# Fewer filler matmuls on TensorE at eight places of a two-layer diffusion block

## The reference

```python
for layer in range(DEPTH):                                   # DEPTH = 2
    mod_l = silu(c) @ w_mod[layer] + b_mod[layer]            # six vectors: shift, scale, gate, twice
    y_l, y_c = mixer(modulate(x, sh1, sc1), modulate(ctx, csh1, csc1), w_in[layer], ...)
    x = post_norm(x, g1 * y_l, ln1_w[layer], ln1_b[layer])
    x = post_norm(x, g2 * swiglu(modulate(x, sh2, sc2), w_gate_up[layer], w_down[layer]), ...)
    # the context tokens likewise, in layer 0 only
# mixer: h @ w_in, split into global attention, window attention, Fourier mixing, retention;
#        their results side by side, @ w_out
# modulate(x, shift, scale) = layer_norm(x) * (1 + scale) + shift
# post_norm(x, y, w, b) = layer_norm(ALPHA * x + y, w, b)
```

## Time and profile before

| | |
|---|---|
| median of 3 runs | 1728.65 us (1728.42 to 1732.66) |
| the profiled execution | 1728.65 us, of which the span is 1726.8 us |
| TensorE busy | 1648.3 us, 95% |
| GpSimd, VectorE, ScalarE busy | 853.3, 826.3, 454.1 us |
| mean granted TensorE clock | 0.992 |
| mean DMA rate | 94 GB/s |

### The profile page before, as it was taken

How to read it: one execution, slowest core, us unless ns; L and a number is a source line. 1 busy time by engine, 2 the same in 40 slices (tenths; PEclk the granted TensorE clock), 3 DMA queues, 4 the chain that set the end, 5 groups by cost and what they waited for, 6 DMA issues and landing times. The chain is left out here.

```text
span 1726.8 us, 23654 instructions
## 1 busy us (share of the span) xinstructions
PE 1648.3 (95%) x9480; PEld 1391.7 (81%) x9480; DVE 826.3 (48%) x1236; ACT 454.1 (26%) x945; POOL 853.3 (49%) x840
## 2 busy tenths in 40 slices
PE   6999999999899999999999999999999999999997
PEld 4877866767899987899998788786768888688885
DVE  4353254647772415444445684635477421520048
ACT  5511465423500021100003164126433300210021
POOL 4443143623464443544444581523475577587772
PEclk9999999999999999999999999999999999999999
DMA  9212043311353312244642120210013542233321
GB/s 359 76 50 73 2 130 129 109 57 53 98 159 98 110 43 67 64 144 120 198 159 76 67 74 25 73 50 8 26 52 98 147 146 92 92 98 98 98 85 49
DMA packets 157010, 161.98 MB, mean 94 GB/s; under 512 B 6382, under 2 KB 111966, under 8 KB 156646
## 3 DMA queue, kind: packets, MB, share of 16 engines
q1 hardware_dynamic: 136566, 121.40, 22.8%
q10 hardware_dynamic: 20336, 39.08, 6.9%
HBM read 158.36 MB, written 2.10 MB: 93 GB/s over the span
## 5 line engine op out<-in xcount | busy, mean ns | idle before, releaser
L675 POOL TENSOR_SCALAR ring_hi<-stage 128x512 fp32r<-128x512 f32 x352 | 247.9, 704 | 621.4 <-PE ps L745 595.0
L678 POOL TENSOR_TENSOR ring_lo<-stage,ring_hi 128x512 fp32r<-128x512 f32 x352 | 490.0, 1392 | 29.4
L743 PE MATMUL ps<-act_hi,ring_hi 128*128 128x384 f32 (+2 forms) x1088 | 379.9, 349 | 0.0
L745 PE MATMUL ps<-act_hi,ring_lo 128*128 128x384 f32 (+2 forms) x1088 | 378.3, 348 | 0.0
L744 PE MATMUL ps<-act_lo,ring_hi 128*128 128x384 f32 (+2 forms) x1088 | 378.2, 348 | 0.0
L743 PE MATMUL ps<-ring_hi,act_hi 128*128 128x512 f32 (+1 forms) x700 | 280.7, 401 | 11.6 <-DVE act_lo L1872 5.4
L745 PE MATMUL ps<-ring_hi,act_lo 128*128 128x512 f32 (+1 forms) x700 | 273.3, 390 | 0.0
L744 PE MATMUL ps<-ring_lo,act_hi 128*128 128x512 f32 (+1 forms) x700 | 273.1, 390 | 0.0
L745 PEld LDWEIGHTS ps<-act_hi,ring_lo 128*128 128x128 f32 x1088 | 204.6, 188 | 13.2
L743 PEld LDWEIGHTS ps<-act_hi,ring_hi 128*128 128x128 f32 x1088 | 204.7, 188 | 13.0
L744 PEld LDWEIGHTS ps<-act_lo,ring_hi 128*128 128x128 f32 x1088 | 204.7, 188 | 12.9
(11 more groups left out here) (258 smaller groups left out, 2123.3 us busy)
## 6 DMA issues: line engine op xcount, KB each, us to landing
stage<-in_w_gate_up_dram SPq DMA_DIRECT2D x88, 512.0 KB, 5.1
mod_stage<-in_w_mod_dram ACTq DMA_DIRECT2D x56, 512.0 KB, 4.4
stage<-in_w_in_dram SPq DMA_DIRECT2D x18, 1024.0 KB, 5.0
stage<-in_w_down_dram SPq DMA_DIRECT2D x16, 1024.0 KB, 4.9
stage<-in_w_mod_dram SPq DMA_DIRECT2D x12, 1024.0 KB, 5.2
start_mod<-in_w_mod_dram SPq DMA_DIRECT2D x8, 1024.0 KB, 12.3
stage<-in_w_down_dram SPq DMA_DIRECT2D x8, 768.0 KB, 4.4
stage<-in_w_out_dram SPq DMA_DIRECT2D x16, 256.0 KB, 4.5
```

Source lines behind the costliest of these rows:

```text
L675: nc.gpsimd.tensor_scalar(hi_, stage[:, par, j * 512:(j + 1) * 512], 1.0, 0.0, ALU.mult, ALU.add).then_inc(w_hi, 1)
L678: nc.gpsimd.tensor_tensor(lo_, stage[:, par, j * 512:(j + 1) * 512], hi_.bitcast(F32), ALU.subtract).then_inc(w_ready, 1)
L743: nc.tensor.matmul(o, a_hi, b_hi, start=first, stop=False)
L745: return nc.tensor.matmul(o, a_lo, b_hi, start=False, stop=last)
```

## The change

The counts of all eight fillers are cut: 30 to 10, 28 to 10, 18 to 5, 44 to 10 twice, 28 to 8, 30 to 8, 44 to 16. In layer 1's attention the filler also waits for the second exponential instead of the first, and writes bank 7 instead of bank 5. In all, 266 fillers become 77. No other instruction changes on any engine.

```diff
@@ project
                             if n == 0 and j in (4, 7):
-                                keep_clock(1, 44)
+                                keep_clock(1, 10)
...
                 if l == 0:
-                    keep_clock(2, 30)
+                    keep_clock(2, 10)
@@ attention
                     if s == 2 and l == DEPTH - 1:
-                        need(pe, "probs_ready", l, 1)
-                        keep_clock(5, 28)
+                        need(pe, "probs_ready", l, 2)
+                        keep_clock(7, 8)
...
                     if s == 1 and l < DEPTH - 1:
-                        keep_clock(6, 28)
+                        keep_clock(6, 10)
...
                     if s == 2 and l < DEPTH - 1:
-                        keep_clock(6, 18)
+                        keep_clock(6, 5)
@@ gate_up
                     for n in ([1, 2] if n_parts == 2 else []):
-                        keep_clock(0, (30, 44)[n - 1])
+                        keep_clock(0, 8 * n)
                         transposes(key, n)
```

## The result

The changed kernel took 1741.41 us (median of 7 runs, 1737.09 to 1743.81), the kernel before 1732.11 us beside it (7 runs, 1727.55 to 1732.83). The ratio is 1.0057 with a 95% interval of 1.004 to 1.0075: slower, by 9.3 us between the medians. The forecast was 1734.2 us with a range of 1729 to 1739. The direction was right; the size and the range were not.

The account below looks back on a forecast made before the run. The prediction took the kernel as bound by TensorE, busy 95% of the span. Terms of 1.2, 0.7, 0.6, 1.1, 1.8 and 0.2 summed to 5.6 us on 1728.65, giving 1734.2 us, range 1729.0 to 1739.0.

Parts of the forecast that it names:

- No gain from fewer fillers: At all eight places, 189 fillers fewer save 21 us of TensorE work, which all turn into idle time.
- A fall at each place: Clock falls expected at start, both attentions and project; gate_up falls already, with little new there.
- rival 1: Only long gaps lower the clock, so start and attention hold; project 1.8 and gate_up 0.2 remain: 1730.7 us, chance 0.28.
- 3 (nothing happens): Rival: the few fillers suffice at every place, 1728.7 us, chance 0.07.
- Rival 4: Three VectorE steps on the norm chains (project, gate_up) get 0.7 us shorter each: 1726.5 us, chance 0.05.
- start: Program start, 20 fillers fewer, 2.7 us idle: a fall into dense matmuls adds 1.2 us, from 0 to 3.2.
- layer 0's attention: Two gaps, 2.6 and 1.9 us idle: slower scores on the path add 0.7 and 0.6 us, 0 to 1.6 each.
- layer 1's project: Two gaps, 4.5 and 5.2 us idle: slower transposes and products add 1.8 us, from 0.4 to 3.
- layer 1's attention: Two idle pieces of about 1.8 us: a fall into the scores at 1179.35 adds 1.1 us, from 0 to 1.6.
- gate_up: Gaps of 3.1 and 5.3 us idle, the second's fall already present and hidden: adds 0.2 us, from -0.3 to 1.
- what a fall costs: A fall wholly in dense matmuls costs 1.6 us; one over a tile's eight transposes costs 0.7 us.
- Rival 2: Low clock stays longer: start, project and one attention gap meet two low stretches each, 4.8 us more: 1739 us, chance 0.10.

Follow-up runs that it names:

- e3_project: Kernel before with only layer 1's project fillers cut (44 to 10, twice): 1734.88 us, ratio 1.0007.
- e8_gates: Kernel before with the gate broadcasts cut into two pieces, a weight slot's products between them: 1738.95 us, ratio 1.004.
- f1_changed: The changed kernel run again beside the kernel before: 1740.0 us, ratio 1.0042.
- e1_start: Kernel before with only the filler at the program's start cut (30 to 10): 1734.47 us, ratio 1.0004.
- e2_att0: Kernel before with only layer 0's attention fillers cut (28 to 10, 18 to 5): 1735.47 us, ratio 1.0011.
- e5_gateup: Kernel before with only layer 1's gate_up fillers cut (30 to 8, 44 to 16): 1733.49 us, ratio 1.0006.
- e6_more: Kernel before with more fillers at each of the eight places, such as 30 to 33 and 44 to 62: 1733.02 us, ratio 1.0007.
- e4_att1: Kernel before with only layer 1's attention filler changed (28 to 8, bank 7, behind the second exponential): 1733.41 us, ratio 1.0002.

## Why the prediction was wrong, and where it was right

**No gain from fewer fillers: right where the clock was up.** Behind every shortened filler the same engine ended the wait. Its working missed one case: when the clock is already low, 30 fillers take 5.49 us and are themselves on the path (e3_project). The changed kernel does not pay that, which offsets a part of what its own fall costs at the start.

**A fall at each place: right.** All five have low stretches in both profiles of the changed kernel, rivals 1 (short gaps hold) and 3 (nothing happens) did not come. Gaps of 2.61 and 2.56 us, and two of about 1.8 around eight fillers, were enough. By that the idle-gap rule of the Trainium skill, "TensorE: Matmul & The Clock Gate", section "Why this matters for your kernels", which rival 1 followed and whose limit lies above them, does not hold for these gaps. But the start fell in three of seven traces with its 30 fillers too, so a fall there is not the cut's alone. Rival 4, faster by freeing VectorE, did not come either. L1938 in the changed kernel (line, shapes, count, busy us, mean ns, idle) takes what it took; its 1.98 us is still there at 1341.95 and 1350.63:

```profile
L1938 DVE SCALAR_TENSOR_TENSOR resid<-resid,st,bc 128x1024 f32<-128x1024 f32 x20 | 31.3, 1567 | 0.7
```

The row in the trace of before has the same 31.3 us and 1567 ns.

**The price: the terms were too small.** The table sets the prediction's terms beside the difference of the two groups of traces (the place cut as in the change, three traces; the place with its fillers of before, seven traces: the kernel before twice, e8_gates and the single edits of other places), each by the start of the same instructions as above:

| place | predicted | cut: mean (values) | kept: mean | difference |
|---|---|---|---|---|
| start | 1.2 | 2.9 (2.9, 3.0, 2.7) | 1.3 | 1.6 |
| layer 0's attention | 1.3 | 2.4 (1.9, 3.3, 2.0) | 0.2 | 2.2 |
| layer 1's project | 1.8 | 2.2 (2.4, 1.5, 2.8) | 0.6 | 1.6 |
| layer 1's attention | 1.1 | 1.8 (1.8, 1.8, 1.8) | 0.3 | 1.6 |
| gate_up | 0.2 | 0.2 (0.5, 0.0, 0.0) | 0.0 | 0.1 |
| sum | 5.6 | 9.5 | 2.4 | 7.1 |

7.1 us agrees with f1_changed's 1.0042 (7.3 us); it lies near the lower end of the first measurement's interval (6.9 us). Two of the project values, 2.7 kept and 2.8 cut, were followed by 1.4 us given back at 1098, so that place's difference has a fall's uncertainty in it. So has the start's: 1.6 of e1_start's 3.0 us and the 1.3 of e8_gates are lateness of the first `act_lo` from work ahead of the filler, and without both the difference there is 1.2. The agreement to a few tenths is in part luck.

The step that failed is "what a fall costs". It took 1.6 us as the price of one fall, from a stretch of 3.4 us, and let it begin anywhere in the gap. In the changed kernel's two traces the stretches at the start and in both attentions were 6.8 us long, so they reached the work behind the gap in full: 2.7 us behind the start's gap in either trace, 1.8 in layer 1's attention. Where the stretch was 3.4 us, in e1_start, the gap cost 1.4 us, near the term of 1.2. Why most are longer stays open: e3_project has 6.8 us at the start with TensorE busy all through. Rival 2 had this mechanism with a chance of 0.10 and 1739 us. The largest miss is layer 0's attention, where the scores and all transposes up to the next pair ran at the lower clock.

**The base was wrong.** The forecast added its sum to 1728.65 us, the profiled execution and the median of three. Over 82 executions the average is 4.0 us above that. The kernel before pays a part of the same falls in most executions: 2.4 to 2.7 us at the start in three of the seven traces (1.3 in a fourth came from ahead of the filler), and 1.4 to 2.7 us at another place now and then (e2_att0 at layer 1's attention, e5_gateup at project, e8_gates at both layer 0's attention and project). So of the 7.2 us between 1741.4 and the forecast, 3.5 are the base (1732.11 in that set) and 3.7 the effect. Of these 3.7, the places account for 1.5 (7.1 beside 5.6); the rest lies within that measurement's interval (6.9 to 13 us). The range leaned on the same base; 3.5 us higher it would have held 1741.4.

Open: the single edits' times add up to about 5 us (4.8 by averages, 5.4 by medians) and the whole to 7. The intervals (about 2 us to either side of each) allow both, and I did not separate noise from an interaction between places. What sets the clock's behaviour beyond that is not settled by these runs.

## What to carry to other kernels

Filler work in idle time looks free to cut, and by the waits it is; its worth is in the clock, and must be read as the time of the work behind the gap at either clock. If fillers are to be few, make them dense: 77 of 512 columns lost 1.4 us (its interval includes no loss) where 77 of 128 columns lost 7 to 9. A single profile shows one arrangement of the falls, so before adding a few us to a base take more executions than three, and compare the profiled one with them.

## What the runs showed of the hardware

- The mean granted clock of each execution is recorded. Twice its shortfall from 1, times the span, is the time at the lower level: 36 to 40 us on average in the kernel before, 73 to 74 in the changed one. That is about 35 us more at half clock. Had dense work on the path filled it, half of it, some 18 us, would be lost; it cost 7. The rest met idle time or other engines' chains.
- Apart from those cut off by the end of the span, every low stretch in these traces lasted 3.4 us or two, three or four times that, and the same kernel has them at different places in different executions.
- The clock also fell while narrow fillers ran, with no idle time since the first of them: at 31.4 us in e3_project, where they began at 30.16, and at 1180.0 us in e6_more, where they began at 1177.87.
- Broadcast matmuls of 3 rows keep TensorE busy without a gap for 3.9 us, and the clock fell behind the ones near 645 us in all 13 traces that have them in one piece, behind those near 382 us in all but one (e4_att1); the earlier trace rows has the latter in the kernel before. In the changed kernel's trace the broadcast at 382 and the low stretch behind it:

```profile
382.14 4.65 PE L833 MATMUL ps<-mod_row,sel 3*128 3x512 f32 x8
```
```profile
385.20:392.00 6.80, 6.80 (x15) 0.51 0.59 160
```
